# Products of 512 columns in one matmul instead of two in a float32-split encoder kernel

## The reference, cut to what matters

```python
for l in range(DEPTH):
    x = x + 0.5 * rms_norm(swiglu(rms_norm(x, g[FFN1_PRE]), ffn_w_in[l, 0], ffn_w_out[l, 0]), g[FFN1_POST])
    proj = rms_norm(x, g[MIX_PRE]) @ w_in[l]
    ...
    x = x + rms_norm(y @ w_out[l], g[MIX_POST])
    xa = memory_cross_attn(rms_norm(x, g[XA_PRE]), rms_norm(mem, g[XA_MEM]), xa_wq[l], xa_wkv[l], xa_wo[l])
    x = x + rms_norm(xa, g[XA_POST])
    x = x + 0.5 * rms_norm(swiglu(rms_norm(x, g[FFN2_PRE]), ffn_w_in[l, 1], ffn_w_out[l, 1]), g[FFN2_POST])
```

## Time and profile before

| | us |
|---|---|
| median of 3 runs | 2333.51 |
| lowest and highest | 2327.44 and 2343.26 |
| profiled execution | 2346.55 |
| its span | 2344.7 |
| its TensorE busy time | 2315.1 |

### The profile page before, as it was taken

How to read it: one execution, slowest core, us unless ns; L and a number is a source line. 1 busy time by engine, 2 the same in 40 slices (tenths; PEclk the granted TensorE clock), 3 DMA queues, 4 the chain that set the end, 5 groups by cost and what they waited for, 6 DMA issues and landing times.

```text
span 2344.7 us, 46707 instructions
## 1 busy us (share of the span) xinstructions
PE 2315.1 (99%) x19270; PEld 2260.2 (96%) x19270; DVE 1565.0 (67%) x2191; ACT 1064.3 (45%) x1765; POOL 114.6 (5%) x185
## 2 busy tenths in 40 slices
PE   7999999999999999999999999999999999999998
PEld 7999999997999999999999999989989999999998
DVE  7999437646365499993499983475364654999833
ACT  5444335228454364452354452452284544544422
POOL 0000000600000000000000000017000000000000
PEclk9999999999999999999999999999999999999999
DMA  4333323340234133233232332243302441332332
GB/s 140 108 117 122 111 82 135 82 138 19 73 118 144 46 121 113 104 102 100 73 128 107 107 110 97 72 137 90 130 9 74 144 127 40 118 110 103 115 96 76
DMA packets 66258, 236.54 MB, mean 101 GB/s; under 512 B 8882, under 2 KB 10632, under 8 KB 65600
## 3 DMA queue, kind: packets, MB, share of 16 engines
q1 hardware_dynamic: 57600, 209.74, 26.8%
q0 software_dynamic: 8224, 24.12, 3.3%
q10 hardware_dynamic: 288, 0.59, 0.1%
HBM read 232.29 MB, written 2.12 MB: 100 GB/s over the span
## 4 chain that ended last, share of the span: by engine, by line
PE 96%; ACT 2%; DVE 1%; issue 1%; DMA 0%; DVEq 0%; SPq 0%; ACTq 0%
PE bank L399 14%; PE bank L403 14%; PE bank L401 14%; PE bank L503 11%; PE bank L505 11%; PE bank L504 11%; PE bank L652 4%; PE bank L455 3%; PE bank L456 2%; PE bank L457 2%; PE bank L627 2%; PE bank L723 1%; PE bank L440 1%; PE bank L612 1%; PE bank L588 1%
## 5 line engine op out<-in xcount | busy, mean ns | idle before, releaser
L313 DVE TENSOR_TENSOR wl<-raw,wh 128x1024 fp32r<-128x1024 f32 x232 | 285.8, 1232 | 374.7 <-ACT wh L308 374.4
L308 ACT ACTIVATE wh<-raw 128x1024 fp32r<-128x1024 f32 x232 | 245.0, 1056 | 499.1 <-PE bank L403 444.7
L399 PE MATMUL bank<-wh,hs 128*128 128x256 f32 x1408 | 279.0, 279 | 0.0
L403 PE MATMUL bank<-wh,hs 128*128 128x256 f32 x1408 | 278.6, 279 | 0.0
L401 PE MATMUL bank<-wl,hs 128*128 128x256 f32 x1408 | 278.1, 279 | 0.0
L503 PE MATMUL bank<-uH,wh 128*128 128x256 f32 x960 | 268.8, 280 | 0.0
L504 PE MATMUL bank<-uL,wh 128*128 128x256 f32 x960 | 268.5, 280 | 0.0
L505 PE MATMUL bank<-uH,wl 128*128 128x256 f32 x960 | 268.5, 280 | 0.0
L399 PEld LDWEIGHTS bank<-wh,hs 128*128 128x128 f32 x1408 | 214.2, 188 | 0.2 <-issue 0.2
L401 PEld LDWEIGHTS bank<-wl,hs 128*128 128x128 f32 x1408 | 214.3, 187 | 0.0
L403 PEld LDWEIGHTS bank<-wh,hs 128*128 128x128 f32 x1408 | 214.2, 188 | 0.0
(11 more groups left out here) (273 smaller groups left out, 6125.6 us busy)
## 6 DMA issues: line engine op xcount, KB each, us to landing
raw<-in_w_proj SPq DMA_DIRECT2D x128, 512.0 KB, 3.5
raw<-in_w_first SPq DMA_DIRECT2D x96, 512.0 KB, 3.7
raw<-in_w_second SPq DMA_DIRECT2D x88, 512.0 KB, 3.5
side<-in_w_first SPq DMA_DIRECT2D x40, 512.0 KB, 3.6
raw_value<-in_w_first SPq DMA_DIRECT2D x40, 512.0 KB, 4.3
gain_rows<-in_grow POOLq DMA_DIRECT2D x15, 512.0 KB, 5.0
strip<-bias_of_distance POOLq DMA_DIRECT2D x2, 2688.0 KB, 10.8
strip<-in_rpb POOLq DMA_DIRECT2D x96, 24.0 KB, 2.3
```

What stands on the lines that cost most here:

```text
L308: e.activation(wh[u % RING][:], raw[u % RAWS][:], ACT.Copy).then_inc(high_ready, 1)
L313: e.tensor_tensor(wl[u % RING][:], raw[u % RAWS][:], wh[u % RING][:].bitcast(F32), ALU.subtract).then_inc(split_ready, 1)
L399: e.matmul(b[:, c], still_h, hi[:, c], start=first and c.start == 0, stop=False)
L403: mm = e.matmul(b[:, c], still_l, hi[:, c], start=False, stop=last and c.stop == n)
```

## The change

`products` gets a further argument, `step`, the number of columns of one matmul. `unit` passes the smaller of n and 512, `memory_values` 512 and `out_tile` 512. So a product with 512 moving columns is one matmul, into a whole PSUM bank of 512 float32; a product with 256 (the key units) stays as it was. `first_units` and `factor_product` are not touched.

```diff
-            def products(b, still_h, still_l, hi, lo, n, first, last):
+            def products(b, still_h, still_l, hi, lo, n, first, last, step):
 
-                halves = [slice(c, c + HALF) for c in range(0, n, HALF)]
+                halves = [slice(c, c + step) for c in range(0, n, step)]
                 for c in halves:
                     e.matmul(b[:, c], still_h, hi[:, c], start=first and c.start == 0, stop=False)
...
                     mm = products(bank[dest], wh[u % RING][:, cut], wl[u % RING][:, cut], rH(k), rL(k), n,
-                                  k == 0, k == DT - 1)
+                                  k == 0, k == DT - 1, min(n, T))
...
-                        mm = products(b, hi, lo, wh[u % RING][:, cut], wl[u % RING][:, cut], KVW, k == 0, k == DT - 1)
+                        mm = products(b, hi, lo, wh[u % RING][:, cut], wl[u % RING][:, cut], KVW, k == 0, k == DT - 1,
+                                      KVW)
...
                     mm = products(bank[2 * i + c], tH(j)[:, still], tL(j)[:, still], wh[u % RING][:, move],
-                                  wl[u % RING][:, move], T, j == 0, j == n - 1)
+                                  wl[u % RING][:, move], T, j == 0, j == n - 1, T)
```

## The result

| us | before | after |
|---|---|---|
| median of 11 runs each | 2333.42 | 2324.97 |
| lowest and highest | 2327.44 and 2344.1 | 2317.48 and 2327.44 |
| profiled execution | 2346.55 | 2327.44 |
| its span | 2344.7 | 2325.6 |

The ratio is 0.995 with a 95% interval of 0.9929 to 0.997: half a per cent faster, inside what the text ahead called no change. The forecast was 2261, its range 2240 to 2296. The 72.7 us of gain that it had worked out came in as 8.5 between the medians and 19.1 between the two profiled executions, two single executions of kernels whose times spread over 17 us before and 10 after.

What follows compares the result with a forecast made beforehand. The prediction took TensorE to be bound by its own stream of loads and matmuls. Merging was to save 76.7 us, less 4 for waits, 72.7 us: from 2333.51 to 2261 us, range 2240 to 2296.

Steps and rivals of the forecast that it cites:

- I take 215.6 ns for the new matmul, by L723: Merged 512-column matmuls in `products`: assumed pitch 215.6 ns, taken from a plain float32 row with 256 columns.
- upper bound of 226.6: Highest pitch in ns allowed for the merged matmul: no gain over a pair at the better level, 2 x 113.3.
- the sum's term of 76.7 us: Gain from merging: 792 pairs at the better level save 8.7 us, 3432 at the worse save 68.0 us.
- The excess of 4 to 9 ns per matmul belongs to short matmuls that each bring a load: TensorE's 256-column matmuls: time over 109.0 ns was put down to weight loads, which a 512-column stream would hide.
- Rival 2: Excess belongs to the columns: each merged pair gains only one start's 2.3 ns; 2328 us, chance 0.09.
- Rival 1: Excess stays with each matmul at every change of weights: merged pitch 219.9 to 224.3 ns; 2295 us, chance 0.12.
- Rival 3: Untouched 256-column stages change their level: 22 us less (2239) or 7 us more (2268); chance 0.10.
- Rival 4: Loads no longer hidden behind long matmuls, each paying 334 ns: 423 us slower, 2757 us; chance 0.04.
- the point of 233.8: Merged pitch in ns, the mean pair before, from which the change would no longer pay.
- the 3.5 allowed: Gain lost to waits at seven stage boundaries, 0.5 us each, as ACT and DVE have work queued there.
- The 0.24 worked out ahead: Gain in us turning into wait for DVE's uL at each boundary, since two tiles ahead of it get shorter.
- The assumption that the median follows the profiled execution: The gain reckoned on the profiled 2346.55 us was taken equally off the median of 2333.51 us.

Runs made afterwards that it cites:

- m1_forms: Small kernel computing nothing of the reference: TensorE rows of 48 matmuls in many forms; float32r pitch 226.7 ns at 512 columns, 120 at 256.
- b_again: The kernel before, without any edit, profiled again to see whether stages change their pitch levels; 2340.45 us.
- e_units512: The changed kernel with output tiles put back to 256 columns, only units and memory values merged; 2338.72 us, ratio 0.9966 to the kernel before.
- m2_starts: Small kernel: rows of 48 float32r matmuls behind different openings and in the kernel's product orders; 120.0 ns at 256 columns, 226.7 to 227 at 512.
- b_zero: The kernel before with ALIGN 122 for 106, activations' parts 16 floats further; 2402.33 us, ratio 1.0254 to the kernel before.

## Why the prediction was wrong

**The step that failed** is "I take 215.6 ns for the new matmul, by L723". The measured pitch is 228.9 in output tiles and 233.3 in units, above even the upper bound of 226.6, so the sum's term of 76.7 us came in as 16.7 by the stages. That bound had taken for granted that one matmul can't cost more than two. L723 was the wrong row twice over: its 215.6 is the pitch of a record, of which a plain float32 matmul has two, and it belongs to a type that doesn't have this kernel's excess. The Trainium skill (TensorE: Matmul & The Clock Gate, Back-to-back issue gap), weighed there too, has the gap of a matmul, its load not counted, at its columns at 2.4 GHz and 2.5 ns more. By m1_forms the trace agrees for bf16, 215.8 and 109.2 with a load for each matmul, and disagrees for every float32r row. That L723's pitch agreed with this rule was a coincidence of numbers: it set one of two records of a 256-column matmul beside the rule's 512 columns.

**"The excess of 4 to 9 ns per matmul belongs to short matmuls that each bring a load"** is refuted for 512 columns by m1_forms and the stretches after: even the load's record of 188 ns has 40 ns to spare there, and the excess over the bare stream is 13.3 ns at distance 0, as at 256 columns, and 15.6 to 20 in the kernel, more than before. At 256 columns the load does have a part in it (120.0 falls to 113.3 with half a load), but a longer stream doesn't win it back. The argument was by elimination, from a pair of types, with no row of 512 full-width float32r columns in the trace.

**The rivals.** Rival 2, the columns' own price, had 0.09 and named 2328: closest of all, in part by luck. Its price, 2.3 ns a pair whatever the level, holds for units at the worse level (2.1); output tiles gained 6.5 there, and at the better level both lost. What it has right is that the second 256 columns bring an excess of their own: 256 columns have 6.7 or 11.1 ns, 512 have 15.6 or 20. The argument that I held against it, "whole stretches sit at one exact level whatever DVE, ACT and DMA do", speaks only against traffic as the cause, and the other, 112 ns for 256 further columns, was read from durations, which aren't pitches. Rival 1, an excess for each matmul, is right at distance 0: 13.3 ns at 256, 320, 384 and 512 columns alike (448 have 16.0, 272 have 12.0). Rival 3 came true in part beside it: the last network's factor stage went to 113.3 and gave 7.0 us. b_again shows that this happens from execution to execution without any change. Rival 4 didn't come about; still, the units' 233.3 is only 0.5 under the point of 233.8 that it named.

**The sum again, with measured pitches.** Output tiles: 528 pairs 226.6 to 228.9, 2352 pairs 235.4 to 228.9: +1.2 - 15.3 us. Units: 264 pairs 226.6 to 233.3, 888 pairs 235.4 to 233.3: +1.8 - 1.9 us. Together -14.2, where the stages show 15.6 less; the 192 pairs of the memory values add 1.1 by their stages. The units' part is nothing, as e_units512's stages say.

**What held.** The number of matmuls; the duration, 396 ns; one single pitch, gone the two levels, in output tiles and units (not in the memory values). The waits came out smaller than allowed: those for uL rose from 3.3 to 4.1 us, of which 2.6 stand at the program's start in both. What is left are three of the seven boundaries, those ahead of the three later networks, where 0.26 us became 0.50 each; one more has a new wait of 0.2 for `wl`. That is 0.9 us in place of the 3.5 allowed. The 0.24 worked out ahead is met at these three, but by luck: its reason, two tiles shorter by 0.23 us, gives only 0.07 at the pitch found, and the other 0.17 is uL starting 3.01 in place of 2.85 us after the turn, behind DVE's earlier work. No other engine came out. The assumption that the median follows the profiled execution failed: the profiled execution of before, 2346.55, had drawn the worse level in three factor stages and in most of the output. That the faster executions had drawn fewer of them is likely, but they have no trace.

## What to carry to other kernels

Take the pitch of a form from a row of the same data type, width and operand places, and count how many records one matmul has there; if the trace has none, a small kernel with that row costs less than the argument. Where a stretch of one code shows two exact pitches, look at the distance between the moving and the stationary operand in SBUF modulo 256 bytes before counting on a merge, a longer stream or less loading. And where such levels exist, know the kernel's spread before giving a change credit: here it is 30 us, and the change was worth 8.5.

## What was not expected of the hardware

- At the full clock (granted 1.00 in all stretches shown) float32r matmuls back to back are apart by one column a cycle (0.417 ns, from 384 to 512 columns in m1_forms) and an excess: 6.7, 11.1 or 13.3 ns at 256 columns (113.3, 117.8, 120.0), 13.3, 15.6 or 20 at 512 (226.7, 228.9, 233.3). Bf16 has 2.5 (109.2, 215.8).
- At shifts by multiples of 64 bytes the excess depends on the moving less the stationary address modulo 256 bytes: at 0 the pitches are 120.0 and 226.7, at 64 bytes 117.8 or 113.3, and 228.9, at 128 bytes 118.7 and 232.4, at 192 bytes 113.3 or 117.8, and 233.3. One exception: the kernel's memory values, 512 columns at 64 bytes, run at 228.9 or at 233.3, as the key units ahead of them run at 113.3 or 117.8 (ten stages of ten).
- At 64 bytes the level at 256 columns is set at the start of a row and kept: one matmul of 32 or 96 columns ahead gives 113.3, one of 192 or 240 gives 117.8. The kernel's factor stages, at 192 bytes, keep theirs for up to 190 us. At 0 no opening changes anything (m2_starts), and b_zero's runs differ by 0.7 us in 2402.
- A plain float32 matmul stands as two records and takes 431.6 ns at 256 columns, 858 at 512.
- Why a distance costs what it costs, and what in a stage's start decides when nothing is placed there, stays open: no run looked at it. So does why the four sets of runs of the kernel before had medians from 2333.42 to 2349.78; the last three are from three different chips, which was not looked at as a cause.
